# A hybrid attention and convolution trunk on one core: all of the input projection computed with tokens on partitions

## What is computed

```python
h = rmsnorm(x, norm_mix_g[l])
proj = h @ w_in[l]          # 1024 x 5120
q, k, v, c_b, c_c, c_u, g_attn, g_conv = jnp.split(proj, split_idx, axis=-1)
# widths 512, 512, 512, 512, 512, 512, 1024, 1024
q = (q * q_scale).reshape(B, T, N_HEADS, 2, HEAD_DIM)      # 4 heads, 2 x 64
k = k.reshape(B, T, N_HEADS, 2, HEAD_DIM)
attn = diff_attention(q1, q2, k1, k2, vh, rel_bias, lam)
attn = rmsnorm(attn, subln_g[l], SUBLN_EPS) * (1.0 - lambda_init)
y_attn = attn.reshape(B, T, ATTN_W) @ w_branch_attn[l]
y_conv = (c_b * causal_depthwise_conv(c_c * c_u, conv_w[l])) @ w_branch_conv[l]
merged = jax.nn.sigmoid(g_attn) * y_attn + jax.nn.sigmoid(g_conv) * y_conv
x = x + merged @ w_out[l]
```

## Time and profile before

| what | value |
|---|---|
| median of three runs | 1072.42 us |
| span of the profiled execution, first to last instruction | 1069.1 us |
| PE busy | 1061.2 us, 99% |
| DVE, ACT, POOL busy | 70%, 56%, 18% |
| granted PE clock | 0.999 of full speed |
| mixer up to the branch products, layer 0 | 190.84 to 310.13 us |
| the same, layer 1 | 718.41 to 837.68 us |

### The profile page before, as it was taken

How to read it: one execution, slowest core, us unless ns; L and a number is a source line. 1 busy time by engine, 2 the same in 40 slices (tenths; PEclk the granted TensorE clock), 3 DMA queues, 4 the chain that set the end, 5 groups by cost and what they waited for, 6 DMA issues and landing times.

```text
span 1069.1 us, 16546 instructions
## 1 busy us (share of the span) xinstructions
PE 1061.2 (99%) x5380; PEld 901.1 (84%) x5380; DVE 748.7 (70%) x950; ACT 596.7 (56%) x859; POOL 190.7 (18%) x347
## 2 busy tenths in 40 slices
PE   9999999999999999999999999999999999999997
PEld 7888888888889888888888888888888988888886
DVE  6766657868788866665776666668787887676654
ACT  7555445555775755444555544445657666455463
POOL 0354320000250022230002223000004400222300
PEclk9999999999999999999999999999999999999999
DMA  7888886655796687875668787566558967878862
GB/s 243 261 262 243 244 266 200 204 167 162 219 318 200 203 248 243 244 235 189 198 206 250 242 243 225 179 216 190 149 165 258 292 221 223 251 241 253 272 235 79
DMA packets 205223, 238.92 MB, mean 223 GB/s; under 512 B 17940, under 2 KB 179520, under 8 KB 205040
## 3 DMA queue, kind: packets, MB, share of 16 engines
q1 hardware_dynamic: 189968, 198.82, 59.6%
q0 software_dynamic: 14800, 38.86, 12.1%
q10 hardware_dynamic: 400, 0.51, 0.1%
HBM read 218.46 MB, written 19.67 MB: 223 GB/s over the span
## 4 chain that ended last, share of the span: by engine, by line
PE 98%; DMA 0%; ACT 0%; SPq 0%; DVE 0%; issue 0%; DVEq 0%
PE acc L1658 21%; PE acc L1639 17%; PE acc L1640 17%; PE acc L1641 17%; PE acc L1667 11%; PE acc L1734 2%; PE acc L1736 2%; PE acc L1737 2%; PE acc L1662 1%; PE acc L1857 1%; PE mixed L1662 1%; PE score L1662 1%; PE acc L1858 1%; PE acc L1859 1%; PE acc L1615 1%; DMA raw<-in_ffn_w_up_dram 0%
## 5 line engine op out<-in xcount | busy, mean ns | idle before, releaser
L1083 DVE TENSOR_TENSOR w_lo<-raw,w_hi 128x1024 fp32r<-128x1024 f32 x382 | 455.4, 1205 | 224.9 <-ACT w_hi L678 224.0
L678 ACT CAST w_hi<-raw 128x1024 fp32r<-128x1024 f32 (+1 forms) x381 | 390.8, 1037 | 307.8 <-PE acc L1641 201.1
L1639 PE MATMUL acc<-w_hi,xm 128*128 128x512 f32 x816 | 319.2, 391 | 0.0
L1641 PE MATMUL acc<-w_lo,xm 128*128 128x512 f32 x816 | 317.8, 390 | 0.0
L1640 PE MATMUL acc<-w_hi,xm 128*128 128x512 f32 x816 | 317.8, 389 | 0.0
L1658 PE MATMUL acc<-hm,w_hi 128*128 128x512 f32 x656 | 206.2, 396 | 0.0
L1641 PEld LDWEIGHTS acc<-w_lo,xm 128*128 128x128 f32 x816 | 153.2, 188 | 32.0
L1639 PEld LDWEIGHTS acc<-w_hi,xm 128*128 128x128 f32 x816 | 153.2, 188 | 31.8 <-issue 0.2
L1640 PEld LDWEIGHTS acc<-w_hi,xm 128*128 128x128 f32 x816 | 153.3, 188 | 31.3
L1667 PEld LDWEIGHTS acc<-hm,w_lo 128*128 128x128 f32 x720 | 133.3, 188 | 29.0
L540 POOL DMA_DIRECT2D hid_scratch<-sum x176 | 96.3, 554 | 341.5 <-DVE sum L1185 339.7
(11 more groups left out here) (192 smaller groups left out, 884.1 us busy)
## 6 DMA issues: line engine op xcount, KB each, us to landing
raw<-in_ffn_w_gate_dram SPq DMA_DIRECT2D x176, 256.0 KB, 3.1
raw<-in_ffn_w_up_dram SPq DMA_DIRECT2D x176, 256.0 KB, 3.7
raw<-in_ffn_w_down_dram SPq DMA_DIRECT2D x164, 256.0 KB, 3.5
raw<-in_w_in_dram SPq DMA_DIRECT2D x160, 256.0 KB, 3.4
hid_scratch<-sum POOLq DMA_DIRECT2D x176, 64.0 KB, 3.1
part<-hid_scratch POOLq DMA_DIRECT2D x44, 256.0 KB, 3.6
raw<-in_w_out_dram SPq DMA_DIRECT2D x32, 256.0 KB, 3.8
gate_scratch<-acc_lo POOLq DMA_DIRECT2D x64, 64.0 KB, 3.3
```

The costliest lines, as they stand in the source:

```text
L678: nc.scalar.copy(w_hi[:, s, 0:tiles, :], raw[:, s, 0:tiles, :]).then_inc(hi_split, 1)
L1083: nc.vector.tensor_tensor(w_lo[:, s, 0:tiles, :], raw[:, s, 0:tiles, :], w_hi[:, s, 0:tiles, :], ALU.subtract).then_inc(lo_split, 1)
L1639: nc.tensor.matmul(s[:, t, :], xh, wh[:, k], start=not u and not k, stop=False, skip_group_check=True)
L1641: mm = nc.tensor.matmul(s[:, t, :], xh, wl[:, k], start=False, stop=(u, k) == (GU_UNITS - 1, GK - 1), skip_group_check=True)
```

## The change

The queries, keys and the three conv sets are computed like the gates: one set of four units with tokens on partitions for each, and one helper for every set on each engine. ACT scales by `rstd_tok` (`set_of_tokens`), DVE turns two halves (`turn_set`), POOL writes eight DMAs (`half_written`) and reads back. For queries and keys it reads back in two DMAs of 256 KB (`shuffle_heads`), one for each two heads, for a conv set in one of 512 KB. ACT puts the query blocks in token order with two copies. The keys are not put in order: the score products read them as they lie, in runs of 32 tokens. The conv sets are read as blocks by the two DVE multiplications that use them. The values become an ordinary set of four units. `mean_square` now comes after the fourth unit of queries. The staging tile of ACT's copy is the store of `sums` instead of `ffn_store`, and the heads' loops on ACT and DVE are written out.

```diff
-        sums = [sb(f"sum{s}", [PAIR, SEQ]) for s in range(ACCS)]
+        by_token_at = sb("by_token_at", [ACCS * PAIR, SEQ])
+        sums = [by_token_at[:, s * PAIR:(s + 1) * PAIR, :] for s in range(ACCS)]
...
-        gate_turned_at = [v[:, :, :].rearrange("p k n -> p (k n)") for v in acc_lo]
+        set_tok = by_token_at.rearrange("p k n -> p (k n)").rearrange("p (q k t n) -> p q k t n", q=2, k=PAIR, t=QT)
+        set_turned_at = [v[:, :, :].rearrange("p k n -> p (k n)") for v in acc_lo]
+        queries = proj[:, 0:N_HEADS, :]
+        query_raw, key_raw = (v.rearrange("p k n -> p (k n)") for v in (
+            gates[:, KT:KT + N_HEADS, :], proj[:, N_HEADS:2 * N_HEADS, :]))
+        conv_raw = [v.rearrange("p k n -> p (k n)") for v in (conv_b, gates[:, 0:4, :], gates[:, 4:KT, :])]
         gate_raw = [v.rearrange("p k n -> p (k n)") for v in (
...

-                two_sets(l, w_in, 0, w_in, COLS, in_turn=True)
-                two_sets(l, w_in, 2 * COLS, w_in, 3 * COLS)
-                by_token(w_in, l, 2 * QK_W)
-                with loop(sp, QKV_ITERS + CONV_HEADS, {split: 4}, QKV_ITERS) as i:
-                    two_sets(l, w_in, i * (2 * COLS), w_in, i * (2 * COLS) + COLS)
+                for col in (QUERY_COL, KEY_COL, VALUE_COL, *CONV_COLS):
+                    by_token(w_in, l, col)
                 for g in range(GATE_SETS):
                     by_token(w_in, l, GATE_COL + gate_tile(g) * P)
...
+            def half_written(to, j):
+
+                sets_turned.add()
+                sets_out.add(16 * QUARTERS)
+                pool.wait_ge(set_turned, sets_turned.now)
+                for a in range(QUARTERS):
+                    pool.dma_start(to.rearrange("(b i) (j a f) -> j a i b f", b=QUARTERS, j=2, a=QUARTERS)[j, a],
+                                   set_turned_at[j][a * QUARTER:(a + 1) * QUARTER, :].rearrange(
+                                       "i (b f) -> i b f", b=QUARTERS)).then_inc(set_out, 16)
+
+            def shuffle_heads(to, back_at, back_sems):
+
+                half_written(to, 0)
+                half_written(to, 1)
+                pool.wait_ge(set_out, sets_out.now)
+                for j in range(2):
+                    cols = slice(j * PAIR * SEQ, (j + 1) * PAIR * SEQ)
+                    pool.dma_start(back_at[:, cols], to[:, cols]).then_inc(back_sems[j], 16)
+
...
+            def shuffle_mixer(layer):
+
+                if layer > 1:
+                    pool.wait_ge(gates_done, GATE_SETS * (layer - 1))
+                shuffle_heads(query_dram, query_raw, query_back)
+                shuffle_heads(key_dram, key_raw, key_back)
+                if layer == 1:
+                    lam_made()
+                for n in range(3):
+                    shuffle_set(conv_dram[n], conv_raw[n], conv_back[n])
                 for g in range(GATE_SETS):
-                    for j in range(2):
...
+                def set_of_tokens(*needs):
+
+                    units_done.add(GU_UNITS)
+                    wait(act, (used, units_done.now), (acc_summed, sets.now + ACCS), (set_turned, 2 * turned_sets.now),
+                         *needs)
+                    turned_sets.add()
+                    for t in range(QT):
+                        nc.scalar.activation(set_tok[:, :, :, t], acc[sets.fixed % ACCS][:, t, :].rearrange(
+                            "p (q k n) -> p q k n", q=2, k=PAIR), ACT.Copy, scale=rstd_tok[:, t:t + 1]).then_inc(set_by_token, 1)
+                    sets.add()
+
...
-                sets.add(QT)
+                hi()
+                norm_root()
+                hi()
+                set_of_tokens((rstd_turned, norm.now))
+                hi()
+                hi()
+                set_of_tokens()
+                hi()
+                hi()
+                for j in range(2):
+                    wait(act, (query_back[j], 16 * (l + 1)))
+                    nc.scalar.copy(in_quarters(queries[:, j * PAIR:(j + 1) * PAIR, :]),
+                                   set_by_channel(query_raw)[:, j]).then_inc(query_ready, 1)
+                hi()
+                hi()
+                units_done.add(GU_UNITS)
+                wait(act, (used, units_done.now), (acc_summed, sets.now + ACCS))
+                if l == 0:
+                    act.wait_ge(rows_stored, 16)
+                for t in range(QT):
+                    nc.scalar.activation(v_tok[:, t, :], acc[sets.fixed % ACCS][:, t, :], ACT.Copy,
+                                         scale=rstd_tok[:, t:t + 1]).then_inc(v_scaled, 1)
...
+                def turn_set():
+
+                    turned_sets.add()
+                    wait(dve, (set_by_token, QT * turned_sets.now))
+                    dve.sem_inc(acc_summed, 1)
+                    sets.add()
+                    for j in range(2):
+                        wait(dve, (set_out, sets_out.now))
+                        nc.vector.transpose(
+                            set_turned_at[j].rearrange("p (b m n) -> p b m n", b=QUARTERS, m=QT * PAIR),
+                            set_tok[:, j].rearrange("p k t (b n) -> p b (k t) n", b=QUARTERS)).then_inc(set_turned, 1)
+                    sets_out.add(2 * 16 * QUARTERS)
+
...
+                norm_start()
+                lo()
+                norm_rstd()
                 to_tokens()
+                lo()
+                turn_set()
+                lo()
+                lo()
+                turn_set()
                 for _ in range(4):
                     lo()
-                sets.add(QT)
+                wait(dve, (v_scaled, QT * (l + 1)))
+                dve.sem_inc(acc_summed, 1)
...
+                turn_set()
+                lo()
+                wait(dve, (conv_back[1], 16 * layers.now), (conv_back[2], 16 * layers.now))
+                for j in range(2):
+                    last = nc.vector.tensor_tensor(
+                        in_quarters(conv_in[:, j * PAIR:(j + 1) * PAIR, :]), set_by_channel(conv_raw[1])[:, j],
+                        set_by_channel(conv_raw[2])[:, j], ALU.mult)
...
-                normed_sets(V_ITER)
-                    multiply(acc[(sets.fixed - 1) % ACCS], [xm[:, k, :] for k in range(UK, KT)], False, True)
+                gate_up()
+                mean_square()
+                gate_up()
...
+                key_at = set_by_channel(key_raw)
+                first_by_token()
                 for h in range(HEAD_ITERS):
                     head.add()

+                    if h % PAIR == 0:
+                        pe.wait_ge(query_ready, 2 * l + h // PAIR + 1)
+                        pe.wait_ge(key_back[h // PAIR], 16 * (l + 1))
                     for sm in range(2):
                         half = slice(sm * HEAD_DIM, (sm + 1) * HEAD_DIM)
-                        q, k = proj[half, h, :], proj[half, N_HEADS + h, :]
+                        q, k = queries[half, h], key_at[half, h // PAIR, h % PAIR]
                         nc.tensor.matmul(score[:, sm, 0:SEQ], q[:, P:SEQ], k, start=True, stop=True)
-                        mm = nc.tensor.matmul(score[:, sm, SEQ:KEYS], q[:, 0:P], k[:, 0:P], start=True, stop=True)
+                        mm = nc.tensor.matmul(score[:, sm, SEQ:KEYS], q[:, 0:P], k[:, 0], start=True, stop=True)
```

More of the change, by code:

```diff
@@ L910, in _ @@
                 ffn(l == 0)
[L911 to L921 removed]
+                def set_of_tokens(*needs):
[7 more added lines that the diff above has]
+                    sets.add()
+                for _ in range(GU_UNITS):
+                    hi()
+                hi()
[21 more added lines that the diff above has]
+                sets.add()
                 have_table(ACT.Exp)
@@ L1513, in _ @@
                 lo()
-                turn_gates()
-                nc.vector.tensor_tensor(conv, conv, conv_b, ALU.mult).then_inc(conv_ready, 1)
+                turn_set()
+                wait(dve, (conv_back[0], 16 * layers.now))
+                for j in range(2):
+                    c_at = in_quarters(conv[:, j * PAIR:(j + 1) * PAIR, :])
+                    last = nc.vector.tensor_tensor(c_at, c_at, set_by_channel(conv_raw[0])[:, j], ALU.mult)
+                last.then_inc(conv_ready, 1)
                 lo()
```

240 lines of the change are left out of this document (62 added, 178 removed).

## The result

The changed kernel takes **1084.26 us** (median of four runs, 1083.51 to 1085.23); beside it the kernel before took 1072.01 (four runs). The ratio is 1.0115, 95% interval 1.0103 to 1.0127: 12.2 us slower. Forecast were 1073.9 and a range to 1079.5. The sign was that of the likeliest case, the size was not, and the time lies outside the range.

What follows compares the result with a forecast made beforehand. PE, busy 99% of the span, was taken to bound the kernel. Saving 3.3 us and waiting 4.8 for the keys gave +1.5 on 1072.4, so 1073.9 us; range 1069.1 to 1079.5.

Steps and rivals of the forecast that it cites:

- the likeliest case: PE waits 2.4 us for the keys at head 0 of each layer; 1073.9 us, own range 1072.9 to 1074.5, chance 0.40.
- What PE saves: PE's 20 units per layer changing to token form save 1.3 us, values 0.37; 1.67 a layer, 3.3 for both.
- DVE and ACT cost nothing: Token sets on ACT (1.26 us) and DVE (1.30) make PE wait nowhere in the heads; costed at nothing.
- keys in runs of 32: Score products reading keys in runs of 32 floats: taken as nothing, at most a doubling, 6 us for eight heads.
- Step 1: PE stands at the scores at T + 35.8 us, T being the first query product.
- Step 2: After the norm and ACT's scaling of the queries, POOL's first write comes at T + 18.7 us.
- Step 3, the leg: Queries, from POOL's first write to the read back: 7.4 us, so read back at T + 26.1.
- Step 4, the second leg: Keys' half tiles written only after the queries' writes: ready at T + 27.2, another 7.4 us leg to T + 34.6.
- Step 5: Reading 256 KB of keys back, from issue to consumer: 3.6 us, keys there at T + 38.2.
- own bounds for the wait: PE's wait per layer: 1.9 us with legs 7.3, read back 3.3; 6.7 with legs 9.2, read back 4.3.
- The long legs: Rival: POOL's serial queue before the first score, legs 8.5, read back 4.0, wait 5.0 a layer; 1079.1 us, chance 0.30.
- The fall of the clock: Rival: PE's clock halves in the new wait, 2.7 us more a layer, 1079.3; chance 0.07, with slow key reads.

Runs made afterwards that it cites:

- half waits: The change with the two half tiles' landings counted apart, each half turned and read back once its own four writes landed; 1072.14 us, ratio 1.0000 to before.
- lighter loads: The change with only 64 of each row's 512 columns loaded for the weights of values and all three conv sets; 1072.23 us.
- first halves first: The change with keys' own buffer, halves counted apart, and POOL reading first halves of queries and keys before the second halves; 1070.24 us.

## Why the prediction was wrong

**What held.** *What PE saves*: 1.67 a layer was forecast, 1.54 measured in the mixer without a wait (117.75), and 1.05 of 1.15 for the conv units and values. The rule of the Trainium skill, "TensorE: Matmul & The Clock Gate", section "Back-to-back issue gap", by which 20 units would save 0.2, is not borne out: the 8 units of queries and keys alone saved 0.5. *DVE and ACT cost nothing; keys in runs of 32*: the scores of head 1 take 0.86 us to the next product, just as before (227.69 to 228.55; the prediction's 0.7 was the length of the first row alone), and there is no other wait of PE over 1 us. *Step 1*: T + 35.8, measured 35.85. *Step 2*: first write T + 18.7, measured 19.0 in both layers. The place of the wait, and that only it matters, held as well.

**Step 3, the leg**, failed first. I took 7.4 us, the short leg of the earlier trace rows, because the DMA share of the whole stretch was 0.61. It was 8.0 in layer 0 and 8.95 in layer 1. In layer 1 POOL's pause of 2.36 us lies in it. I had that pause in the earlier trace rows and used it only as an argument for a chance. In layer 1 this leg was off by more (1.55) than the second (1.34), and it is not a fixed number: the three profiles with this order of DMAs give 8.95, 9.3 and 10.3 in layer 1.

**Step 4, the second leg**, failed most over the two layers: 7.4 forecast, 9.16 and 8.74 measured. By then ACT has waited 3.9 us for the queries and DVE 4.7 for `set_out`, and when both have gone on DMA is at a share of 0.89 to 0.96 from 221 to 227 (windows as above):

```profile
218.00:221.00 3.00, 3.00 (x15) 2.50 (x14) 2.17 (x3) 0.33 (x1) 1.91 (x4) 1.00 0.17 61
221.00:224.00 3.00, 3.00 (x15) 2.49 (x14) 1.38 (x2) 1.59 (x3) 3.00 (x7) 1.00 0.89 244
224.00:227.00 3.00, 3.00 (x15) 2.46 (x14) 2.36 (x2) 2.98 (x5) 0.55 (x2) 1.00 0.96 342
```

The mean share of a stretch said nothing of this: it was 0.61 before and 0.65 after (192 to 215). The trace of before had part of the burst, in the same windows counted from T: shares of 0.26, 0.91 and 0.57, where these are 0.17, 0.89 and 0.96, and 0.98 in the next. So the lull and the first 3 us of burst come without any wait. What is new is that DMA then stays full; POOL's own 64 KB writes are a part of that, and that the waits of ACT and DVE bunched the loads is the likely rest, argued and not shown. *Step 5*: 3.6 forecast, 3.8 and 3.7 measured. The sum of layer 0 is then 0.3 (start) + 0.6 (first leg) + 1.8 (second leg) + 0.2 (read back) = 2.9 us later than T + 38.2: T + 41.1. In layer 1 it is 0.3 + 1.55 + 1.34 + 0.1 = 3.3: T + 41.5. The wait was 5.1 and 5.4 in place of 2.4. That lies within the prediction's own bounds for the wait (1.9 to 6.7); the range was cut at a wait of 5.0.

**The rivals were added wrongly.** The long legs were given 5.0 of wait and 1079.1 us, and that wait is what came. The fall of the clock was priced at 2.7 a layer and happened, with 2.6 and 1.9 (2.1 and 3.0 in the change run again). With the long waits alone the time would have been some 1079.8, just above the range (1079.5); the clock put another 4.5 us on it. But I had made them two cases of 0.30 and 0.07 that exclude each other. I had written that a long wait might not leave the clock full, so the case of long legs was itself the case of the slow clock: 1079.1 + 5.4 = 1084.5. The range had to reach there. Counted from the rows, the two mixers give -3.1 saved, +10.5 waited and +4.5 of clock, 11.9 us, where their lengths give 11.8.

## What to carry to other kernels

Where a new wait stands in PE's way, price it with the clock behind it, as one case: here waits of 5.1 and 5.4 us cost 7.6 and 7.3, and in a second run waits of 4.9 and 5.6 cost 7.0 and 8.6. Take the price of a DMA chain from rows whose DMA is as busy as the chain's own moments, not from the mean of the stretch, and ask whether the waits of the change may bunch the loads it will run beside. And a shuffle through DRAM that stands behind another one on one queue should first lose what ties the two together (the shared buffer, the shared count): a buffer and a count of its own alone turned 12 us of loss into a gain of 1.7 here. But giving up this part of the change gave 3.0 on the same chip, and the best version with the shuffle only came level with that.

## What the runs showed that was not expected

**A wait's length did not decide alone whether the clock fell.** After a wait of 2.2 us (half waits, layer 1) it was full, after one of 1.9 (lighter loads, layer 1) it was half, though PE had been busy again for 0.4 us when it fell. That cost 1.6 us. Windows of the two, from the wait on:

```profile
753.80:756.00 2.20, 0.07 (x1) 0.00 (x0) 0.98 (x1) 2.20 (x4) 0.20 (x1) 1.00 0.51 204
756.00:758.00 2.00, 1.92 (x13) 1.66 (x14) 2.00 (x3) 1.98 (x3) 0.35 (x1) 1.00 0.34 111
```

```profile
753.40:755.40 2.00, 0.06 (x2) 0.04 (x2) 0.00 (x0) 1.99 (x4) 0.00 (x0) 1.00 0.81 271
755.40:757.40 2.00, 2.00 (x10) 1.68 (x11) 0.62 (x1) 0.45 (x1) 0.00 (x0) 0.61 0.09 22
757.40:759.40 2.00, 2.00 (x6) 1.54 (x6) 1.93 (x5) 0.37 (x2) 0.00 (x0) 0.54 0.00 0
```

It fell in all six waits of 4.0 to 5.6 us that were left idle, and in none of those of 1.2 or less. In between, these two cases are all there is. In the seven falls the clock went down between 2.4 and 5.0 us after the last product ahead of the wait.

**POOL's pause of 2.36 us** keeps to a place in POOL's program. It comes behind the third write of layer 1's mixer, whichever set that is: the queries in the change (748.66), the first conv set with queries and keys in channels (770.79), the first gate set before. It never comes behind the third write of layer 0's mixer. In the version with first halves first layer 1 (118.68) is 0.94 longer than layer 0 (117.74): 0.56 of it is the later start of the scores, 0.15 a remainder right behind them, and the pause is the likely cause of both. What causes the pause stays open; no run was made to move it.
